# A relative-bias table made early: its row, its write and its reads moved to the weight queue

## The reference: two transformer blocks over 256 tokens

```python
mq, mk, mv, nq, kc, vc, ksl, vsl, kwn, vwn, gz = split(rmsnorm(x) @ w_in)
# 8 MoBA heads, 8 NSA heads in 2 groups; each branch adds a bias by distance:
s_own = q @ k.T * scale + table[head, rel_bucket(t - s)]        # MoBA, own block
k_cmp = silu(blocks(kc) @ cmp_k_w1) @ cmp_k_w2                  # compressed keys (v alike)
s_cmp = nq @ k_cmp.T * scale + table[head, rel_bucket(d_cmp)]   # every 16th key
s_s, s_w = the selected and the window branch, with the same table
```

## Time and profile before

| | |
|---|---|
| three runs | 1185.88, 1186.72, 1189.43 us; median 1186.72 us |
| span of the profiled execution | 1183.5 us (3.2 us less than the median of the runs) |
| TensorE busy | 1169.2 us, 99% of the span |
| VectorE busy | 833.2 us, 70% |
| ScalarE busy | 664.0 us, 56% |
| GpSimd busy | 214.6 us, 18% |
| DMA | 206.05 MB, mean 174 GB/s |
| bias table: write | 1 DMA of 384 KB on ACT's queue |
| bias table: reads | 16 DMAs of 128 KB on ACT's queue |

### The profile page before, as it was taken

The page is one execution under the profiler, slowest core; times in us unless marked ns, Lnnn a source line. Parts: engine busy times, 40 slices in busy tenths (PEclk is TensorE's granted clock), DMA queues, the critical chain, the costliest instruction groups (busy, mean ns, idle before and its releaser), DMA issues.

```text
span 1183.5 us, 18540 instructions
## 1 busy us (share of the span) xinstructions
PE 1169.2 (99%) x7440; PEld 1024.3 (87%) x7440; DVE 833.2 (70%) x1269; ACT 664.0 (56%) x1083; POOL 214.6 (18%) x286
## 2 busy tenths in 40 slices
PE   9999999999999999999999999999999999999997
PEld 8886788888898788888888888899998699888886
DVE  7878777766568687666567877547977777777753
ACT  6538666643443666665446555545665865655641
POOL 0106442110000341111101111110002921111100
PEclk9999999999999999999999999999999999999999
DMA  8891345555457234555554554564463123555551
GB/s 309 254 245 40 107 179 202 186 213 193 152 192 285 73 142 178 179 188 204 214 181 147 205 179 169 182 203 161 168 214 141 50 99 128 184 178 183 189 194 76
DMA packets 33654, 206.05 MB, mean 174 GB/s; under 512 B 3856, under 2 KB 6432, under 8 KB 11808
## 3 DMA queue, kind: packets, MB, share of 16 engines
q1 hardware_dynamic: 29840, 200.60, 47.2%
q10 hardware_dynamic: 3728, 4.26, 1.7%
HBM read 203.39 MB, written 1.46 MB: 173 GB/s over the span
## 4 chain that ended last, share of the span: by engine, by line
PE 90%; DVE 3%; ACT 2%; DMA 2%; POOL 1%; issue 1%; ACTq 0%; DVEq 0%; POOLq 0%; SPq 0%
PE ps L684 41%; PE ps L689 22%; PE ps L701 3%; PE ps L702 3%; PE ps L703 3%; PE ps L2059 2%; PE ps L2058 2%; PE ps L2057 2%; DMA raw<-wstream 1%; PE ps L1015 1%; PE ps L756 1%; PE ps L757 1%; PE ps L758 1%; DMA h<-xt 1%; DVE wl L632 1%; PE ps L715 1%
## 5 line engine op out<-in xcount | busy, mean ns | idle before, releaser
L632 DVE TENSOR_TENSOR wl<-raw,wh 128x2048 fp32r<-128x2048 f32 (+4 forms) x190 | 417.2, 2202 | 101.1 <-ACT wh L603 101.1
L603 ACT ACTIVATE wh<-raw 128x2048 fp32r<-128x2048 f32 (+2 forms) x192 | 350.9, 1831 | 126.7 <-PE ps L689 54.0
L684 PE MATMUL ps<-xb,wh 128*128 128x512 f32 x1392 | 333.6, 392 | 0.0
L684 PEld LDWEIGHTS ps<-xb,wh 128*128 128x128 f32 x1392 | 255.6, 188 | 51.0 <-issue 0.8
L684 PE MATMUL ps<-ab,wh 128*128 128x512 f32 x772 | 188.3, 392 | 0.6 <-DVE ab L1081 0.6
L689 PEld LDWEIGHTS ps<-xb,wl 128*128 128x128 f32 x1392 | 178.4, 191 | 6.8
L689 PE MATMUL ps<-xb,wl 128*128 128x256 f32 x1392 | 180.5, 283 | 0.0
L684 PEld LDWEIGHTS ps<-ab,wh 128*128 128x128 f32 x772 | 140.6, 188 | 28.2 <-DVE ab L1081 1.5
L940 DVE TENSOR_TENSOR tf<-ps,tf 128x256 f32<-128x256 f32 x148 | 62.3, 424 | 103.0 <-ACT tf L935 103.0
L935 ACT ACTIVATE tf<-ps 128x256 f32<-128x256 f32 x148 | 56.2, 382 | 121.0 <-PE ps L689 120.7
L689 PEld LDWEIGHTS ps<-ab,wl 128*128 128x128 f32 x772 | 101.1, 191 | 5.1
(11 more groups left out here) (371 smaller groups left out, 1720.2 us busy)
## 6 DMA issues: line engine op xcount, KB each, us to landing
raw<-wstream SPq DMA_DIRECT2D x168, 1024.0 KB, 4.8
raw<-wstream SPq DMA_DIRECT2D x16, 704.0 KB, 4.2
raw<-wstream SPq DMA_DIRECT2D x4, 792.0 KB, 4.2
raw<-wstream SPq DMA_DIRECT2D x4, 512.0 KB, 6.6
e_bt<-scratch ACTq DMA_DIRECT2D x16, 128.0 KB, 8.1
o_bt<-scratch SPq DMA_DIRECT2D x2, 1024.0 KB, 5.8
raw<-wstream SPq DMA_DIRECT2D x2, 560.0 KB, 8.6
raw<-wstream SPq DMA_DIRECT2D x2, 528.0 KB, 3.4
```

Of the source, the lines that this page charges most:

```text
L603: e.g.activation(WH[i % HLN][:, 0:w], RAW[i % RAWN][:, 0:w], ACT.Copy).then_inc(S["hi"], 1)
L632: e.g.tensor_tensor(WL[q][:, 0:w], RAW[i % RAWN][:, 0:w], f32(WH[q][:, 0:w]), ALU.subtract).then_inc(S["lo"], 1)
L684: e.g.matmul(two(PS[p.bank[p.unit(n)]][:, :]), WH[c % HLN][:, at * 128:at * 128 + 128], x2[:, :, tile(ks[k])], start=k == 0, stop=False, s ...
```

## The change

The row is copied by DVE right behind the scaled `r` tile, before the low part of chunk 3. SP issues the write to DRAM, on the queue of the weights, behind the fetch of chunk 6. Then come, on the same queue, the fetches of chunks 7 to 10, and two reads behind each of them; SP waits for the write to land behind the fetch of chunk 7. There are eight reads instead of sixteen: each fills 16 partitions and all 16 heads, 256 rows of 1 KB. ACT issues none of these DMAs any more. One semaphore `bt` stands for the two.

```diff
-        def spread_bias(e, half):
-            e.wait_ge(S["d_scr"], 16)
-            hs = slice(2048 * half, 2048 * half + 2048)
-            for a in range(8):
-                src = bass.AP(scratch.tensor, 8 * half * 16 * 385 + 127 - 16 * a, [[384, 16], [16 * 385, 8], [1, 256]])
-                e.g.dma_start(e_bt[16 * a:16 * a + 16, hs].rearrange("p (h s) -> p h s", h=8), src).then_inc(S[f"bt{half}"], 16)
+        def spread_bias(e, shares):
+            for a in shares:
+                src = bass.AP(scratch.tensor, 127 - 16 * a, [[384, 16], [16 * 385, 16], [1, 256]])
+                e.g.dma_start(e_bt[16 * a:16 * a + 16, :].rearrange("p (h s) -> p h s", h=16), src).then_inc(S["bt"], 16)

         def sp_even(e):
             ...
             sp_gemm(e, G["km"])
+            row = TMP[1][0:16, 0:384]
+            e.wait_ge(S["row"], 1)
+            e.g.dma_start(bass.AP(scratch.tensor, 0, [[16 * 385, 16], [385, 16], [1, 384]]),
+                          bass.AP(row.tensor, row.offset, [list(row.ap[0]), [0, 16], [1, 384]])).then_inc(S["d_scr"], 16)
+            for x in range(4):
+                fetch_to(e, G["km"].first + 4 + x)
+                if x == 0:
+                    e.wait_ge(S["d_scr"], 16)
+                spread_bias(e, (2 * x, 2 * x + 1))

 # act_even
-            e.wait_ge(S["row"], 1)
-            row = TMP[1][0:16, 0:384]
-            e.g.dma_start(... scratch <- row ...).then_inc(S["d_scr"], 16)
             act_gemm(e, G["km"])
             ...
             act_gemm(e, G["qn"])
-            spread_bias(e, 1)
             act_gemm(e, G["ks"])
-            spread_bias(e, 0)

 # dve_even
                 e.g.tensor_tensor(two(TF[2][:, :]), two(PS[p.bank[0]][:, :]), rbx(2), ALU.mult).then_inc(S["ev_dve"], 1)
-                lo_to(e, G["km"].first)
-            def table_row(e, c):
-                lo_to(e, G["km"].first + 1)
                 e.wait_ge(S["table"], 1)
                 e.g.tensor_copy(TMP[1][0:16, 0:384], PS[3][0:16, 0:384]).then_inc(S["row"], 1)
+                lo_to(e, G["km"].first)
             ...
-                     between=table_row)
+                     between=lambda e, c: lo_to(e, G["km"].first + 1))
             ...
-            e.wait_ge(S["bt1"], 128)
+            e.wait_ge(S["bt"], 128)
             ...
-                    e.wait_ge(S[f"bt{h // 8}"], 128)
```

More of the change, by code:

```diff
@@ L394, in stream_no @@
     return 1 + at // 4 if c == 0 else 5 + at // 8 if c == 1 else 5 + c
-SEMS = ("fsum dga dgp iw smv er ct0 ct1 gated iv ptd rl eps psa psb pss pr ysq ysum acc adt ah al blk blkh blkl bt0 bt1 const cq cts cum cva cvd cz d_c d_out d_scr d_v ea "
+SEMS = ("fsum dga dgp iw smv er ct0 ct1 gated iv ptd rl eps psa psb pss pr ysq ysum acc adt ah al blk blkh blkl bt const cq cts cum cva cvd cz d_c d_out d_scr d_v ea "
         "ev_act ev_dve rel low ex fah fal gemm gp gq gs gz h_down0 h_down1 h_eo h_oo hi lam_a lam_d lf lo mh ml mx na "
@@ L1229, in act_even @@
                 e.g.activation(e_blkh[:, sl], blk[i][:, 0:480], ACT.Copy).then_inc(S["blkh"], 1)
-            e.wait_ge(S["row"], 1)
-            row = TMP[1][0:16, 0:384]
-            e.g.dma_start(bass.AP(scratch.tensor, 0, [[16 * 385, 16], [385, 16], [1, 384]]),
-                          bass.AP(row.tensor, row.offset, [list(row.ap[0]), [0, 16], [1, 384]])).then_inc(S["d_scr"], 16)
             act_gemm(e, G["km"])
@@ L1701, in sp_odd @@
             sp_gemm(e, G["oq"])
-            e.wait_ge(S["bt0"], 128)
-            e.wait_ge(S["bt1"], 128)
+            e.wait_ge(S["bt"], 128)
             e.wait_ge(S["cq"], 1)
```

## The result

| | before | after |
|---|---|---|
| median of 5 runs | 1186.72 us | 1200.76 us |
| lowest and highest | 1185.49, 1189.43 us | 1196.99, 1204.78 us |
| span of the profiled execution | 1183.5 us | 1200.2 us |

The ratio is 1.0122, 95% interval 1.0107 to 1.0137. The forecast was 1191.4 us with a range up to 1194.6: slower, as forecast, but three times as much. The changed kernel's profiled execution took 1202.03 us by its own count, 1.8 us more than its span and 1.3 more than the median. The runs of before in the experiments have the same 1.8 us around their spans; so before's profiled execution took about 1185.3 us, 1.4 under its median, and of the 3.2 us that were taken to lie around its span only 1.8 do. These two, 1.3 and 1.4 us, are why the spans differ by 16.7 us and the medians by 14.0.

The account below looks back on a forecast made before the run. TensorE bounds the kernel, busy 1169.2 of 1183.5 us, with the table off the path. Late weight chunks, then DVE's line, delay `kc` by 4.7 us, earlier waits included: 1186.7 + 4.7 = 1191.4 us, range 1187.0 to 1194.6.

Parts of the forecast that it names:

- The row's copy: On DVE ahead of chunk 3's low part: 0.54 us, covered with 0.3 us left, so costing nothing.
- ACT's issues: Write and 16 reads leave ACT: chunk 8's fetch about 0.2 us earlier; the reads' 7.4 us of issuing worth nothing.
- the write: On SP's queue behind chunk 6: 4.2 us of transfer, landing at 36.3 us; chunk 7 after it lands at 38.9.
- rival C: The write lands at 38.5 us, delaying chunk 8's fetch to 40.1: sum 6.9 us, 1193.6 us; chance 0.12.
- 3.15: Microseconds assumed for a pair of merged reads (0.52 MB) on SP's queue, between bounds of 1.3 and 3.3.
- The line of chunks and pairs: Weight queue always full up to chunk 11: chunks 8 to 11 land at 44.75, 50.65, 56.55 and 62.45 us.
- What is late next: Chunk 11's low part on DVE starts 5.1 us later, hidden units at 73.75; TensorE waits at `kc`, 4.7 us behind.
- gives nothing back: After `kc`, chunks 12 to 16 have free engines and nothing new is late, but TensorE is busy throughout and recovers nothing.
- The sum: 4.7 us on the profiled execution, 1183.5 to 1188.2; with 3.2 us around the span unchanged, a median of 1191.4 us.
- The rule of the Trainium skill: DMA engines alternate between queues by packet, each queue in order; on SP's queue a chunk waits for the whole pair ahead.
- A: The reads fit: a pair takes 1.3 us at the weights' 404 GB/s, giving 1187.4 us (1186.7 to 1188.1); chance 0.26.
- B: Not slower: chunk 8 lands up to 1.4 us earlier, TensorE's wait at 48.90 goes, 1185.3 us; chance 0.10.

Follow-up runs that it names:

- e8: The kernel before with only its sixteen reads merged into eight of neighbouring partitions, on ACT's queue at the old places: 1195.6 us, ratio 1.0076.
- e9: e1 with the source addresses of spread reads (step 377) but still filling 16 neighbouring partitions: 1192.36 us, ratio 1.0057.
- e6: The changed kernel with sixteen reads of neighbours, half 1 over all shares, then half 0, so successive reads reach different partitions: 1195.67 us.
- e3: The changed kernel with its reads split into sixteen of 8 heads, each share's two halves in a row, same queue and places: 1198.29 us.
- e5: The changed kernel with each of the eight reads filling every eighth partition instead of 16 neighbours, same queue and places: 1191.7 us, ratio 1.005.
- e4: The changed kernel with small filler matmuls while TensorE waits (50 before chunk 8, 80 before `qn`, 35 before `kc`): 1199.21 us, ratio 1.0113.
- e2: The changed kernel with its eight reads still early but issued on ACT's own queue, behind the splits of chunks 6 and 7: 1198.1 us.
- e10: The kernel before with only its sixteen reads spread over every eighth partition, on ACT's queue at their places: 1184.79 us, ratio 0.9986.
- e1: The changed kernel with its eight merged reads back on ACT's queue at the old places, copy and write as changed: 1194.66 us, ratio 1.0068.
- e7: e1 with each read spread over every eighth partition: 1184.47 us, ratio 0.9987.
- e12: The changed kernel with its pairs of reads behind chunks 11 to 14 on SP's queue, spread over every eighth partition: 1185.98 us, ratio 1.0006.

## Why the prediction was wrong

The place of the delay was right, its size was not. By the prediction's own steps:

- **The row's copy, ACT's issues, the write:** right in the outcome. No wait at 27.4 us, chunk 7 there at 39.3 (forecast 38.9), rival C didn't happen. Two misses offset each other: the write landed 1.7 us sooner than forecast, at 34.6, and chunk 7's fetch went out 1.2 us later, at 32.7.
- **"The pieces stay at 1 KB, so merging changes the count of issues and not of pieces; I take 3.15":** the step that failed. The 160 GB/s had been measured on reads of before, half as large and each to other partitions than the one ahead of it. Merged, twice as many pieces in a row go to the same 16. At the measured 115 GB/s a pair takes 0.524 MB / 115 GB/s = 4.6 us, not 3.15. The reason was in the diff, in the destination `16 * a:16 * a + 16`, and the rate was taken over to a shape that the row did not show. Shown by e8 (the merge alone, 120 GB/s and 9.4 us), e9 (not the source), e6 against e3 (the order) and e5 (the same eight DMAs in the same places, 1191.7 us with the reads spread).
- **The line of chunks and pairs:** right in order, short in size. Four pairs at 4.6 make chunk 11 4 x 1.45 = 5.8 us later than forecast; it was 8.8. The other 3.0 aren't placed as a whole. Part of them is seen where a pair gives way to a chunk: 129 GB/s in 40.5 to 42.5 us. Also in e5 chunk 11 was 0.9 late.
- **What is late next:** right. VectorE's line from chunk 11 to the hidden units kept its 8.8 us, and `kc` waited. It came at 82.7 instead of 73.8, which is chunk 11's 8.8 us and 0.1 more.
- **TensorE "gives nothing back", and no more:** a missing term. The prediction had no clock. Around the gap of 2.25 us at `kc` the granted clock was half for 6.8 us, and the rest of the span took 3.0 us longer; in e4, with the clock up, it took as long as before. That this gap would bring the lower clock wasn't certain: in e2, e3 and e6 it didn't.
- **The sum:** 4.75 + 8.9 (`kc` at 82.71 instead of 73.8) + 3.0 = 16.7 us of span, as measured. The forecast for the median then took the 3.2 us around the span as fixed; only 1.8 of them are.
- **The rule of the Trainium skill ("DMA: Bandwidth & Descriptors") on arbitration:** it was read as a reason why ACT's queue is kinder to the weights. e2 doesn't bear that out. Its chunk 8 landed at 53.7 us instead of 47.1, with no packet of it moved in 40 to 44 us. In the time e2 stands at 11.8 us over before and the change at 14.0, and their intervals overlap.
- **Rivals A and B** needed faster reads and fell with the same step. What was held against A, that the engines were fully busy at 160 GB/s, was no ceiling of the pieces: e10 reads at 212 GB/s with the same pieces. A's 404 GB/s was reached by no read.

The table splits the 14.0 us: merging neighbours costs 9.4 in the old place (e8), the reads' move to the busy stretch another 4.6 (from e8) to 5.7 (from e1). The two don't simply add: unmerged, the move costs 9.5 (e6). With spread reads merging costs nothing (e7 against e10), and the move costs 7.2 (e5 against e7, one chip).

## What to carry to other kernels

Before a DMA's rate is taken from a row, compare which partitions each transfer and its neighbours in the queue reach, not only the size of the pieces; a table that fills 128 partitions in shares of 16 did better here at every eighth partition than in blocks. Small transfers belong where TensorE has weights in hand, and even there a pair in the weights' own queue wasn't safe (e12). A delay that opens a gap of over 2 us in TensorE is to be priced with and without a stretch of half clock behind it, here 3 us. A transfer off the path has slack that ends: say how many microseconds, and what slower version would use it up.

## What the runs showed of the hardware

- Eight reads of 16 x 16 pieces of 1 KB: 111 to 120 GB/s into 16 neighbouring partitions (125 in e2), 186 to 212 into every eighth; the source's step made no difference (114). The DMA engines show as fully busy in each case, so a full share doesn't say what limits.
- Reads of half the size into neighbours reached 160 (before) and 150 to 172 GB/s (e6) when each went to other partitions than the one ahead of it, and 125 (e3) when two in a row went to the same.
- A slow transfer holds up what shares the engines with it. In its own queue 129 GB/s were moved where a pair gave way to weights, against 404 for weights alone. In the other queue nothing of a chunk issued at 38.4 us moved in 40 to 44 us (e2).
- Two queues got equal numbers of packets in 82 to 88 us of e1, so 1 KB pieces beside 8 KB pieces got an eighth of the bytes. In 60 to 66 us of e1 and 40 to 44 us of e2 the shares weren't equal.
- With every gap in TensorE of 2.8 to 10.6 us the granted clock fell to 0.5, for 3.4 us (e4, 54.5 to 57.9) to 10.2 (e1, 89.1 to 99.3). Of the five gaps of 2.2 to 2.4 us at `kc` two had it (the change, e5) and three not (e2, e3, e6). At before's 1.35 us gap it stayed at 1.00.
